# Giving the odd experts' second matrices a place of their own in a 32-expert decoder step

## The reference

```python
hgu = xb @ moe_w_gu[e] + moe_b_gu[e]          # (rows,1024) x (1024,2048)
gate, up = hgu[:, :D_EXPERT], hgu[:, D_EXPERT:]
gate = jnp.minimum(gate, SWIGLU_LIMIT)
up = jnp.clip(up, -SWIGLU_LIMIT, SWIGLU_LIMIT)
act = (up + 1.0) * gate * jax.nn.sigmoid(SWIGLU_ALPHA * gate)
return act @ moe_w_down[e] + moe_b_down[e]    # (rows,1024) x (1024,1024)
```

## Time and profile before

| | us |
|---|---|
| median of 3 runs | 1240.98 (1238.27 to 1241.37) |
| span of the profiled execution | 1236.2 |
| TensorE matmul busy | 1165.1 (94%) |
| VectorE busy | 383.4 (31%) |
| ScalarE busy | 278.6 (23%) |
| weights moved by SP's queue | 447.07 MB |

### The profile page before, as it was taken

The page is one execution under the profiler, slowest core; times in us unless marked ns, Lnnn a source line. Parts: engine busy times, 40 slices in busy tenths (PEclk is TensorE's granted clock), DMA queues, the critical chain, the costliest instruction groups (busy, mean ns, idle before and its releaser), DMA issues.

```text
span 1236.2 us, 16623 instructions
## 1 busy us (share of the span) xinstructions
PE 1165.1 (94%) x6700; PEld 656.6 (53%) x6700; DVE 383.4 (31%) x722; ACT 278.6 (23%) x505; POOL 23.2 (2%) x47
## 2 busy tenths in 40 slices
PE   9999999999999999999999998999999999999995
PEld 8999889985434343435343434344443434343432
DVE  5888588753120202023202020212112020202024
ACT  5686454432102010101010101010111101010101
POOL 1000011000000000000000000000000000000000
PEclk9999999999999999998999999999999999999998
DMA  9735578986999999999999999999999999999993
GB/s 285 236 125 183 164 229 263 360 298 266 427 372 423 426 426 426 426 428 399 382 424 428 427 424 424 425 425 426 428 425 426 426 428 426 427 423 427 425 426 153
DMA packets 82509, 456.97 MB, mean 370 GB/s; under 512 B 6608, under 2 KB 45632, under 8 KB 48960
## 3 DMA queue, kind: packets, MB, share of 16 engines
q1 hardware_dynamic: 79632, 447.07, 89.1%
q0 software_dynamic: 2832, 9.28, 2.4%
HBM read 450.38 MB, written 5.95 MB: 369 GB/s over the span
## 4 chain that ended last, share of the span: by engine, by line
PE 87%; DVE 5%; DMA 3%; ACT 3%; issue 2%; DVEq 0%; SPq 0%; ACTq 0%
PE pool L976 33%; PE pool L899 18%; PE ub L856 8%; PE pool L625 5%; PE pool L626 5%; PE pool L627 5%; PE ob L987 3%; DMA gu_w<-in_moe_w_gu 2%; PE ub L987 2%; ACT arena L1231 1%; PE pool L887 1%; PE pool L915 1%; PE ob L926 1%; PE pool L972 1%; ACT wh L1041 1%
## 5 line engine op out<-in xcount | busy, mean ns | idle before, releaser
L976 PE MATMUL pool<-gu_w,arena 128*64 128x512 f32 x1920 | 421.6, 597 | 0.2 <-DMA gu_w<-in_moe_w_gu 0.2
L976 PEld LDWEIGHTS pool<-gu_w,arena 128*64 128x64 f32 x1920 | 143.1, 138 | 261.9 <-issue 255.0
L899 PE MATMUL pool<-dn_w,arena 128*64 128x512 f32 x992 | 219.6, 595 | 22.5 <-ACT arena L1231 22.5
L1713 DVE TENSOR_SCALAR arena<-pool 128x512 f32<-128x512 f32 x31 | 21.5, 692 | 702.0 <-PE pool L976 697.1
L625 PE MATMUL pool<-xh,wh 128*128 128x264 f32 x568 | 163.8, 288 | 1.6 <-DVE arena L1310 0.6
L627 PE MATMUL pool<-xh,wl 128*128 128x264 f32 x568 | 160.8, 283 | 0.0
L899 PEld LDWEIGHTS pool<-dn_w,arena 128*64 128x64 f32 x992 | 70.8, 137 | 150.5 <-issue 150.5
L1226 ACT ACTIVATE arena<-arena 128x512 f32<-128x512 f32 x32 | 20.1, 630 | 452.2 <-DVE arena L1713 452.2
L625 PEld LDWEIGHTS pool<-xh,wh 128*128 128x128 f32 x568 | 106.9, 188 | 8.5 <-issue 4.4
L626 PE MATMUL pool<-xl_most,wh 128*128 128x264 f32 x385 | 109.2, 284 | 0.0
L627 PEld LDWEIGHTS pool<-xh,wl 128*128 128x128 f32 x568 | 106.5, 187 | 0.0
(11 more groups left out here) (336 smaller groups left out, 794.8 us busy)
## 6 DMA issues: line engine op xcount, KB each, us to landing
gu_w<-in_moe_w_gu SPq DMA_DIRECT2D x124, 2048.0 KB, 15.0
dn_w<-in_moe_w_down SPq DMA_DIRECT2D x124, 1024.0 KB, 11.5
dn_w<-in_w_in SPq DMA_DIRECT2D x24, 1024.0 KB, 5.6
dn_w<-in_w_branch SPq DMA_DIRECT2D x8, 1024.0 KB, 5.7
gu_w<-in_moe_w_gu SPq DMA_DIRECT2D x8, 1024.0 KB, 8.6
gu_w<-in_state_gla POOLq DMA_DIRECT2D x8, 512.0 KB, 6.9
out_gla_sample<-gu_w POOLq DMA_DIRECT2D x8, 512.0 KB, 4.6
dn_w<-in_w_o SPq DMA_DIRECT2D x4, 1024.0 KB, 9.1
```

The source lines that it names most:

```text
L899: last = mm(DOWN[s * CAP:(s + 1) * CAP, :], act_t[:, k % 4, k // 4 * CAP:(k // 4 + 1) * CAP], block[:, s * HF:(s + 1) * HF], start=(k == 0 ...
L976: last = mm(out, xg[:, k, j * CAP:(j + 1) * CAP], gu_w[:, k, cols], start=False, stop=(k == NB - 1))
```

## The change

`early` is named `dn_odd` and holds the second matrix of every odd expert, for good; `dn_w` holds those of the even experts. The arrival semaphores are doubled, four for each home. In SP's order the second matrix of an expert stands ahead of its first, and waits for the expert two before it (`- 2 * NB`). After the loops the last expert's first matrix stands ahead of its second. TensorE's order is the same; `down` reads from the home of its expert.

```diff
-        early = [blocks(slot(i, 0, 2 * D), 2) for i in (5, 3, 6, 0)]
+        dn_odd = [blocks(slot(i, 0, 2 * D), 2) for i in (5, 3, 6, 0)]
...
-        dn_in = [sem(f"dn_in{k}") for k in range(NB // 2)]
+        dn_in = [[sem(f"dn_in_{w}{k}") for k in range(NB // 2)] for w in ("even", "odd")]
...
-                             .rearrange("e (p a) n -> (e p) a n", a=2)).then_inc(dn_in[k], 16)
-
-            def load_early(i):
-
-                sp.dma_start(early[i], w_down[0, 1, 2 * i * P:(2 * i + 2) * P, :].rearrange("(p a) n -> p a n", a=2)
-                             ).then_inc(dn_in[i], 16)
+                             .rearrange("e (p a) n -> (e p) a n", a=2)).then_inc(dn_in[0][k], 16)
+
+            def load_odd(k, e):
+
+                sp.dma_start(dn_odd[k], w_down[0, bass.ds(e, 1), 2 * k * P:(2 * k + 2) * P, :]
+                             .rearrange("e (p a) n -> (e p) a n", a=2)).then_inc(dn_in[1][k], 16)
...
-            def load(n, e):
+            def next_gu(n, e):
 
                 for k in range(NB // 2):
                     sp.wait_ge(gu_used, n * NB + 2 * k + 2 - NB)
                     load_two(k, e)
+
+            def next_dn(n, e, odd):
+
                 for k in range(NB // 2):
-                    sp.wait_ge(dn_used, n * NB + 2 * k + 2 - NB)
-                    load_dn(k, e)
+                    sp.wait_ge(dn_used, n * NB + 2 * k + 2 - 2 * NB)
+                    (load_odd if odd else load_dn)(k, e)
 
             def body(it, pair):
-                load(it * 2 + 1, pair * 2 + 1)
-                load(it * 2 + 2, 0 if pair is PAIRS - 1 else pair * 2 + 2)
-
-            for e in (1, 2):
-                for k in range(NB // 2):
-                    sp.wait_ge(gu_used, (e - 1) * NB + 2 * k + 2)
-                    load_two(k, e)
-            for k in range(NB // 2):
-                sp.wait_ge(dn_used, 2 * k + 2)
-                load_dn(k, 2)
-
+                even = 0 if pair is PAIRS - 1 else pair * 2 + 2
+                next_dn(it * 2 + 1, pair * 2 + 1, True)
+                next_gu(it * 2 + 1, pair * 2 + 1)
+                next_dn(it * 2 + 2, even, False)
+                next_gu(it * 2 + 2, even)
+
+            next_gu(1, 1)
+            next_gu(2, 2)
+            next_dn(2, 2, False)
             at = moe_loops(sp, body)
-            load(at * 2 + 1, E - 1)
+            next_gu(at * 2 + 1, E - 1)
+            next_dn(at * 2 + 1, E - 1, True)
...
-            def down(n, weights=dn_w, count=None):
+            def down(n, it, odd):
 
                 pe.wait_ge(actt_ready, n + 1)
                 pe.wait_ge(eo_ready, n + 1)
                 for k in range(NB):
-                    pe.wait_ge(dn_in[k // 2], count or n * 16 + 16)
-                    block = early[k // 2][:, k % 2, :] if weights is early else weights[:, k, :]
+                    pe.wait_ge(dn_in[odd][k // 2], it * 16 + 16)
+                    block = dn_odd[k // 2][:, k % 2, :] if odd else dn_w[:, k, :]
```

More of the change, by code:

```diff
@@ L449, in _ @@
                     wait_drained(sp, f"b1{NB - 1}")
-                    load_early(0)
+                    load_odd(0, 1)
                 if i == len(tiles) - 5:
@@ L471, in _ @@
                     wait_drained(sp, f"b0{NB - 1}")
-                    load_early(1)
+                    load_odd(1, 1)
                     wait_filled(sp, f"b0{NB - 1}")
@@ L478, in _ @@
             wait_drained(sp, f"wo{NB - 1}")
-            load_early(2)
+            load_odd(2, 1)
             sp.wait_ge(lgt_full, 1)
-            load_early(3)
-            def load(n, e):
+            load_odd(3, 1)
+            def next_gu(n, e):
                 for k in range(NB // 2):
@@ L927, in first_pair @@
                     last.then_inc(gu_used, 1)
-                down(0, dn_w, 32)
+                down(0, 0, 0)
                 turn_act(1)
@@ L933, in first_pair @@
                     gather(half, gath_done)
-                down(1, early, 32)
+                down(1, 0, 1)
             def amid():
@@ L1006, in body @@
                     turn_act(n)
-                    down(n)
+                    down(n, it, j)
                     if final and j == 0:
```

## The result

| | before | after |
|---|---|---|
| median, us | 1240.55 (6 runs, 1238.27 to 1241.37) | 1244.11 (6 runs, 1241.73 to 1245.42) |
| ratio | | 1.0027, 95% interval 1.0017 to 1.0038 |
| span of the profiled execution, us | 1236.2 | 1242.1 |
| clip of expert 0 / 15 / 16 / 31, us | 306.99 / 741.78 / 775.92 / 1206.79 | 308.14 / 742.56 / 782.95 / 1212.85 |

The forecast was 1242.0, range 1238.7 to 1246.3, "same" by the 0.3% bound. The time lies in the range and the slowdown stays under that bound, but its interval excludes "no change": the extra time is 3.6 us instead of 1.0 and has another cause. The profiled execution of after took 1243.87 us, 1.8 more than its span. If that also holds for before, its profile is one of the fastest executions: 1238 against a median of 1240.55.

What follows compares the result with a forecast made beforehand. TensorE was taken to set the pace, with a DMA-bound last pair. Late first matrices at the end (+1.57) less expert 31's vanished wait (0.6) gave +1.0 us on the median 1240.98: 1242.0, range 1238.7 to 1246.3.

Steps and rivals of the forecast that it cites:

- What bounds the kernel: Expert loop: TensorE sets the pace, 57.35 us a pair against 59.1 of transfers; the queue's credit ends at the last pair.
- The 9.86 us of dn(3), both gaps, the deadlines: Transfer queue: dn(3) adds 9.86 us, gaps of 3.93 and 4.37 close, gu(9).k3 meets its deadline by 0.37.
- Four more semaphores and the changed wait constants leave TensorE's list as long as it was: 0: TensorE's instructions: no cost, bounded either way by 0.02 us a step, 0.6 us over 30 experts.
- +1.57 at experts 29 and 30: Loop's end: gu(30).k3 lands 1.56 us later, so expert 30's clip comes 1.57 us later, part already at gu(29).
- -0.6 at expert 31: Last expert: gu(31).k3 lands nine us ahead of its deadline, so the 0.6 us lost to late transfers vanishes.
- The sum: Whole kernel: +1.57 - 0.6 = +1.0 us, giving 1242.0 against the median 1240.98.
- (b): Slower rival: gap at amid stays open, gu(30).k3 lands 5.93 us late; +5.3, 1246.3 us; chance 0.06.
- (c): Rival: TensorE's waits at gu(29) and gu(30) also lower its clock, 1.4 us each; +3.8, 1244.8 us; chance 0.04.
- The limit of about 358 GB/s: HBM loads: by this rule the four extra transfers take 11.7 us, sum +2.8; set aside for the trace's 426 GB/s.
- The sign that was named: Changed profile: a mid-loop clip step other than those forecast (28.43 and 28.9 us) would show the prediction wrong.

Runs made afterwards that it cites:

- e2: The changed kernel with ten waits in TensorE's never-run overflow branch, putting the last loop's entry at 8157 as in before; 1239.96 us, ratio 0.9998.
- g1: The kernel before, with TensorE's pairs from 5 on as one loop of computed length, without the jump; 1241.13 us, ratio 1.0003.
- g2: The changed kernel plus ten never-run waits (e2), with TensorE's pairs from 5 on as one computed loop, no jump; 1240.46 us, ratio 1.0001.
- f2: The changed kernel with four waits (two instructions) in TensorE's never-run overflow branch, last loop's entry at 8154; 1245.15 us.
- g3: g2 with SP requesting each first matrix ahead of its second for every pair from 8 on; 1235.05 us, ratio 0.9955.
- f4: e2 with first matrix requested ahead of second for experts 27 to 30, and amid moved after pair 7, one loop left out; 1246.35 us, ratio 1.0045.

## Why the prediction was right, and where it was not

The measured time lies in the range, and below 0.3%. But the step that carries the time was missing, and the one that was to carry it did not happen in after. That the range holds 1244.11 is in part luck: 1242.0 came from waits that are absent, and the room above it had been left for rivals that did not come true. The small slowdown itself shows in the profile of e2 (+0.75) and in no timed run.

- **What bounds the kernel: right.** The pace is TensorE's until the credit of the queue is used up. g1 and g2 show it from the other side: 5.3 us taken from TensorE, nothing gained. In g1 the last eight steps are 5.3 us longer than in before, and the step at `amid` 2.1.
- **The 9.86 us of dn(3), both gaps, the deadlines: right.** Landing times within 1 us of the forecast, gap at `amid` closed (from the landing ahead of it to that of gu(11).k0 594.45 to 599.35, 4.90 us, where it was 9.30), deadline of gu(9).k3 just met (step 28.46 in after; in f2 28.70, so there it was missed by 0.27).
- **"Four more semaphores and the changed wait constants leave TensorE's list as long as it was: 0": the step that failed.** Its bound from the 0.02 us of a regular step was a bound on a body that stays the same. The body lost one register instruction, ahead of the odd expert's second matrix: the idle time of that weight load is 0.86 instead of 0.94, the step 28.83 instead of 28.90. That is a gain of 0.9 us over the loop. And the program has seven such bodies, five of them ahead of the last loop; so its entry moved by five instructions, which costs 6.25 us at expert 16. The prediction put this term at 0 and measured it is +6.25 - 0.9.
- **+1.57 at experts 29 and 30: right as a mechanism, hidden in after.** In e2 it is 2.0: from clip 0, gu(30).k3 lands 1.2 us later than in before (867.7 against 866.5; forecast 1.56), and TensorE wants it 0.8 us earlier. In after TensorE comes to the last experts 6.2 us later than in e2 by its step 16. The same landing is only 4.15 us later (871.9), most of it because the queue ran empty behind the stand: from 772.70 to 780.75 there are 8.05 us between two landings of 2 MiB, 3.1 idle. That leaves 2.1 us of room, just what e2 lacks: step 30 is 28.85 in after. In f2, with a stand like it, the landing is at 872.7, and its step 30, 29.46, has 0.6 us of wait.
- **-0.6 at expert 31: right**, 0.45.
- **The sum.** Forecast +1.0; the profiles have 6.25 - 0.45 - 0.9, +4.9; the medians +3.6, with 2.1 to 4.7 by the interval. The missing 1.3 was not traced to a step. Two things that vary between profiles of unchanged code are of that size: clip 0, by 2.6 us with the dips of the clock in the mixer, and the step at `amid`, 41.04 to 42.74 in the kernels with the old loops.
- **The rivals.** (b) came nearer in size (+5.3) by a mechanism that did not happen: the gap at `amid` did close. (c), lower clock at the waits of 29 and 30, is out: in e2 the window of 1144 to 1148, with TensorE busy 3.14 of 4.00, stands at 1.00. Where idleness was long, at expert 16, the clock did fall, for longer after the longer stand. The limit of about 358 GB/s of the Trainium skill (DMA: Bandwidth & Descriptors, Where 436 GB/s comes from) did not show either: after moves 425 to 426 GB/s in its full stretches, with one core at work, and no run here has two.
- **The sign that was named.** The prediction listed "a clip step other than these in mid-loop" as what would show it wrong. That is what came, at one expert. The rows of before already had the stretch of 3.36 us there, and I used them only for the clock. The question not asked was why TensorE stood idle with no wait at that very place.

## What to carry to other kernels

Where a trace has an engine idle on "issue" at a jump, price it before any edit: its length depends on where the code lies, and an edit that drops one register instruction in a repeated body moved it by 5.3 us here. The same shift changed the median time by 3.6 to 5.7 us. Before a small difference is credited to an edit, compare it with a version that has the same layout (instructions in a branch that never runs will do). When compute and transfers are as close as here (57.3 and 59.1 us a pair), time taken from either one was given back by the other until the order of the transfers was changed too; only g3, which did both, was faster than before by more than 0.3%.

## What the runs showed of the hardware

- TensorE stands for 3.1 to 3.5 us or for 8.0 to 8.9 us at a jump over code that does not run, with nothing between in the places tried; one border lies between entries 8154 and 8157. Entry 8408, 256 places past 8152, behaves as 8152, which fits a rule that repeats every 256 instructions; one point does not prove it. Packets of code come 5.7 to 5.9 us apart there in the fast kernels as in the slow ones; why, stays open, and so does f4's long stretch (entry 7586).
- After the stand of 8.66 us the granted clock is 0.64, 0.50 and 0.58 in three windows of 4 us, against one of 0.66 after 3.36 us, which makes 0.95 us of difference; waits of the weight load in e2, up to 1.7 us, left it at 1.00. Idle stretches alone don't explain it: behind the small matmuls of `amid` it stood at 0.54 from 580 to 584 us in before, with TensorE busy 3.10 of 4.00 and no idle stretch over 0.90 from 555 us on.
- One register instruction fewer ahead of a weight load went with 0.08 us less idle time of the load. The step is 28.82 to 28.84 us instead of 28.90 in all ten kernels with the new homes; the load also reads from another tensor there, and the two were not parted.
- The clock can dip in a busy stretch as well: 0.79 at 224 to 232 us in the profile of after, TensorE busy 7.89 of 8.00, in code that before ran at 1.00. In the 4 us ahead of it TensorE was busy 3.20 of 4.00 in both.
